# Two diffusion-mixer layers on one core: a re-ordered first norm, three first weight tiles instead of two, and prepared tables ahead of the first copies

## The reference

```python
ada_lat = silu_c @ ada_w[l] + ada_b[l]       # 1024 -> 6*1024: shift, scale, gate, twice
ada_ctx = silu_cc @ ada_w[l] + ada_b[l]
h  = rms_norm(x,  lp["ln1"]) * (1.0 + sc1)  + sh1     # latent tokens
hc = rms_norm(xc, lp["ln1"]) * (1.0 + csc1) + csh1    # context tokens
z  = h @ w_in                                # 1536 columns, in 12 tiles of 128
# columns of z: attention (low-rank q, kv, shared rotary key), Fourier, S5 state space
a_bar = exp(dt * a);  b_bar = ((a_bar - 1) / a) * b   # S5 tables: powers of a_bar times b
```

## Time and profile before

| | |
|---|---|
| median of 3 runs | 2171.99 us (2169.01 to 2174.01) |
| profiled execution | 2170.0 us, of which span of the trace 2168.1 us |
| PE | busy 2125.3 us, 98% of the span |
| DVE | 1228.1 us, 57% |
| POOL | 903.7 us, 42% |
| ACT | 505.2 us, 23% |
| mean granted TensorE clock | 0.995 |

### The profile page before, as it was taken

The page is one execution under the profiler, slowest core; times in us unless marked ns, Lnnn a source line. Parts: engine busy times, 40 slices in busy tenths (PEclk is TensorE's granted clock), DMA queues, the critical chain, the costliest instruction groups (busy, mean ns, idle before and its releaser), DMA issues.

```text
span 2168.1 us, 30631 instructions
## 1 busy us (share of the span) xinstructions
PE 2125.3 (98%) x12532; PEld 1897.7 (88%) x12532; DVE 1228.1 (57%) x1859; ACT 505.2 (23%) x814; POOL 903.7 (42%) x492
## 2 busy tenths in 40 slices
PE   6999999999999999999999999999999999999998
PEld 4999999877799899999999999888777787888886
DVE  7998981455663546454565424594266757263353
ACT  3115121454300220110201111322265212010010
POOL 2441443200243354444444443455411456766662
PEclk9999999999999999999999999999999999999999
DMA  7363354233553332122233254545310552322331
GB/s 282 100 141 101 116 191 145 88 120 120 199 192 138 133 122 88 59 78 88 78 88 103 92 204 187 120 153 195 127 39 23 197 182 88 107 97 97 97 97 68
DMA packets 105390, 267.80 MB, mean 124 GB/s; under 512 B 22650, under 2 KB 42490, under 8 KB 103470
## 3 DMA queue, kind: packets, MB, share of 16 engines
q1 hardware_dynamic: 68928, 190.87, 25.9%
q10 hardware_dynamic: 36334, 75.07, 10.5%
HBM read 227.56 MB, written 37.88 MB: 122 GB/s over the span
## 4 chain that ended last, share of the span: by engine, by line
PE 89%; DVE 8%; DMA 1%; ACT 1%; issue 1%; SPq 0%; POOL 0%; DVEq 0%; POOLq 0%; ACTq 0%
PE ps L482 67%; PE ps L1062 3%; PE ps L936 2%; PE ps L1076 2%; PE ps L1112 2%; PE ps L600 2%; PE ps L491 2%; DVE t_out L2233 2%; DVE t_in L2233 1%; PE ps L795 1%; PE ps L962 1%; PE ps L974 1%; PE ps L497 1%; PE ps L1009 1%; PE ps L925 1%; DMA ada_first<-in_ada_w 1%
## 5 line engine op out<-in xcount | busy, mean ns | idle before, releaser
L1304 POOL TENSOR_SCALAR whi<-raw 128x1024 fp32r<-128x1024 f32 x244 | 273.5, 1121 | 1212.1 <-PE ps L482 665.3
L1307 POOL TENSOR_TENSOR wlo<-raw,whi 128x1024 fp32r<-128x1024 f32 x244 | 630.7, 2585 | 20.3
L482 PE MATMUL ps<-hh,whi 128*128 128x384 f32 (+1 forms) x1560 | 462.8, 353 | 0.3 <-DVE ada L626 0.3
L482 PE MATMUL ps<-hl,whi 128*128 128x384 f32 (+1 forms) x1560 | 460.0, 351 | 0.0
L482 PE MATMUL ps<-hh,wlo 128*128 128x384 f32 (+1 forms) x1560 | 459.8, 351 | 0.0
L482 PEld LDWEIGHTS ps<-hh,whi 128*128 128x128 f32 x1560 | 283.6, 188 | 21.1 <-ACT mr L1737 1.0
L482 PEld LDWEIGHTS ps<-hl,whi 128*128 128x128 f32 x1560 | 285.3, 188 | 18.6 <-issue 0.2
L482 PEld LDWEIGHTS ps<-hh,wlo 128*128 128x128 f32 x1560 | 285.0, 188 | 18.4
L2166 DVE SCALAR_TENSOR_TENSOR x<-ps,ada,x 128x384 f32<-128x384 f32 (+1 forms) x160 | 80.5, 546 | 335.1 <-PE ps L482 335.0
L482 PE MATMUL ps<-midh,whi 128*128 128x384 f32 (+1 forms) x768 | 231.3, 355 | 1.8 <-DVE midl L2196 1.8
L482 PE MATMUL ps<-midl,whi 128*128 128x384 f32 (+1 forms) x768 | 229.7, 353 | 0.0
(11 more groups left out here) (259 smaller groups left out, 2954.9 us busy)
## 6 DMA issues: line engine op xcount, KB each, us to landing
raw<-in_w_main SPq DMA_DIRECT2D x244, 512.0 KB, 3.3
ada_gap<-in_ada_w SPq DMA_DIRECT2D x40, 512.0 KB, 10.1
ada_mixer<-in_ada_w SPq DMA_DIRECT2D x32, 512.0 KB, 4.0
g_d<-gt ACTq DMA_DIRECT2D x24, 384.0 KB, 2.4
gl<-g_d ACTq DMA_DIRECT2D x8, 1152.0 KB, 6.2
ada_first<-in_ada_w SPq DMA_DIRECT2D x16, 512.0 KB, 15.4
cout_d<-cz SPq DMA_DIRECT2D x12, 512.0 KB, 5.0
cout<-cout_d ACTq DMA_DIRECT2D x6, 1024.0 KB, 9.3
```

The costliest lines, as they stand in the source:

```text
L482: ins = pe.matmul(bank(p, h, a, b), ww[:, w % W_SLOTS, kw * P:(kw + 1) * P], xx[:, kx, a:b], start=(first and i == 0 and j == 0), stop=(la ...
L1304: pool.tensor_scalar(whi[:, u, :], raw[:, u % 2, :], 1.0, 0.0, ALU.mult, ALU.add).then_inc(w_split.sem, 1)
L1307: pool.tensor_tensor(wlo[:, u, :], raw[:, u % 2, :], whi[:, u, :].bitcast(F32), ALU.subtract).then_inc(w_split.sem, 1)
```

## The change

1. **DMA order.** The S5 input matrix (b_in, 384 KB) leaves the very start and is issued by ACT in the middle of the first norm. Weight tile 2 is loaded ahead of ada steps 12 to 15. Each ada step of the first 16 has a semaphore of its own, not one for two.
2. **Sums.** DVE adds all eight squares; PE sums once (6 matmuls in the program, not 12). PE then runs ada steps 4 to 6, spreads the first 512 tokens, runs step 7 and spreads the rest.
3. **Gain.** The part of the gain that doesn't depend on c, (ada_b + 1) * ln, is formed early (`first_gain_constant`, two small operations); later the sums are multiplied by ln where they lie in PSUM and added to it (`first_gain`, two small operations in place of one).
4. **First part in two pieces.** For k = 0 the first 512 tokens are handed from DVE to ACT and from ACT to PE on signals of their own.
5. **Power table.** Doublings 1 and 2 move from ahead of the first norm to behind its k = 3; doubling 4 moves to behind k = 7. POOL starts the split of tile 2 only after doubling 2.
6. **Three tiles.** PE takes tiles 0 and 1 through k = 0 to 3, with ada steps 8-10, 11-12 and 13-15 behind k = 0, 1, 2 and the turn of the second ada block behind the high part of k = 3; then tile 2 through k = 0 to 3, then tiles 0 to 2 together through k = 4 to 7. Tile 3 uses PSUM region 3, and the waits of tiles 3 to 6 follow.
7. **Copies later.** DVE does `inverses` and `input_weights` ahead of the three `inputs`, and all three of these ahead of `table_rows`.

```diff
-IN_PAIRS = ((0, 1, 2, 0, 1, 2, 0, 1, 2, 0, 1, 0), ...
+IN_PAIRS = ((0, 1, 2, 3, 1, 2, 0, 1, 2, 0, 1, 0), ...
+        def pe_first_sums(pe):
+            key = (0, 1)
+            pe.wait_ge(sq_used.sem, sq_used.at((key, KD - 1)))
+            for b in range(TOK // P):
+                ins = pe.matmul(ps[:, norm_pair(key), 2 * b:2 * b + 2], sqa[:, b * P:b * P + P], ones[:, 0:2], ...
+        def pe_first_spread(pe):
+            pe.wait_ge(diag_ready.sem, diag_ready.at(key))
+            pe.matmul(ps[:, norm_pair(key), 0:512], ones[:, :], diag[:, 0:512], start=True, stop=True)
+            pe_ada(pe, 7)
+            pe.matmul(ps[:, norm_pair(key), 512:TOK], ones[:, :], diag[:, 512:TOK], ...
+            pe_turn(pe, 0)
-            pe.wait_ge(ada_full[slot].sem, ada_full[slot].at(s | 1 if s < 8 * ADA_FIRST else s))
+            pe.wait_ge(ada_full[slot].sem, ada_full[slot].at(s))
+        def first_gain(dve, i):
+            dve.tensor_tensor(o, o, ln[...]..., ALU.mult)        # o lies in PSUM
+            dve.tensor_tensor(g, o, g, ALU.add)
...
 # pe_layer, l == 0
-                for k, steps in ((0, range(8, 11)), (1, range(11, 14))):
-                    first_tiles(range(2), k)
+                for i in range(2):
+                    wait_w(pe, i)
+                    for h, a, b in halves_of(TOK):
+                        pe.wait_ge(hi_ready.sem, hi_ready.at((0, 1, 0) if h else "piece"))
+                        for ww in (whi, wlo):
+                            pe.matmul(bank(i, h, a, b), ww[:, i, 0:P], hh[:, 0, a:b], start=(ww is whi), stop=False)
+                pe.wait_ge(lo_ready.sem, lo_ready.at((0, 1, 0)))
+                for i in range(2):
+                    low_step(pe, i, i, 0, TOK)
+                for k, steps in ((0, range(8, 11)), (1, range(11, 13)), (2, range(13, 16))):
+                    if k:
+                        first_tiles(range(2), k)
                     for s in steps:
                         pe_ada(pe, s)
...
-                for k in range(3, KD):
-                    first_tiles(range(2), k)
-                pe.wait_ge(ada_ready.sem, ada_ready.at(1))
-                tile(2, 2)
-                pe.wait_ge(in_dve.sem, in_dve.at((0, 0)))
-                tile(3, 0)
+                wait_w(pe, 2)
+                pe.wait_ge(ada_ready.sem, ada_ready.at(("gain", 0, 0, 4)))
+                for k in range(4):
+                    first_tiles((2,), k)
+                for k in range(4, KD):
+                    first_tiles(range(3), k)
+                tile(3, 3)
                 pe.wait_ge(in_dve.sem, in_dve.at((0, 1)))
                 tile(4, 1)
+                pe.wait_ge(in_act.sem, in_act.at((0, 3)))
                 halves(0)
...
 # POOL, split
+                if not t0 and u == 2:
+                    pool.wait_ge(prep_dve.sem, prep_dve.at((0, "power", 2)))
...
 # dve_layer, l == 0
                 dve_norm(dve, 0, 1, TOK, 0, KD // 2)
+                doubled(dve, 0, 1)
+                doubled(dve, 0, 2)
+                dve_ada(dve, 1)
+                first_gain(dve, 1)
+                dve_norm(dve, 0, 1, TOK, KD // 2, KD)
                 doubled(dve, 0, 4)
-                dve_ada(dve, 1)
-                dve_gain(dve, 0, 0, KD // 2, KD)
-                dve_norm(dve, 0, 1, TOK, KD // 2, KD)
-                inputs(0)
-                inputs(1)
                 inverses(dve, 0)
                 input_weights(dve, 0)
+                for i in range(3):
+                    inputs(i)
                 table_rows(dve, 0)
-                input_tables(dve, 0, 0)
-                inputs(2)
-                for c in range(1, S5_PARTS):
+                for c in range(S5_PARTS):
                     input_tables(dve, 0, c)
...
 # DVE, at the very start
             coefficients(dve, 0)
-            for k in range(1, KD - 1):
+            for i in range(2):
+                first_gain_constant(dve, i)
+            for k in range(1, 4):
                 add_squares(dve, (0, 1), k, TOK)
             transition(dve, 0)
-            doubled(dve, 0, 1)
+            for k in range(4, KD):
+                add_squares(dve, (0, 1), k, TOK)
             invert(dve, (0, 1), TOK)
-            doubled(dve, 0, 2)
```

More of the change, by code:

```diff
@@ L579, in ada_slot @@
             if s < 8 * ADA_FIRST:
[L580 removed]
+                return ada_first[s], s
             s -= 8 * ADA_FIRST
@@ L797, in chunk_inputs @@
                 ins.then_inc(bu_done.sem, bu_done.mark((l, q)))
-            for i in range(2):
-                wait_w(pe, t0 + i)
+            if l:
+                for i in range(2):
+                    wait_w(pe, t0 + i)
             if l == 0:
-                for k, steps in ((0, range(8, 11)), (1, range(11, 14))):
-                    first_tiles(range(2), k)
+                for i in range(2):
[10 more added lines that the diff above has]
+                        first_tiles(range(2), k)
@@ L1219, in _ @@
                 pe_ada(pe, s)
[L1220 to L1226, removed]
+            pe_first_sums(pe)
+            for s in range(4, 7):
+                pe_ada(pe, s)
+            pe_first_spread(pe)
             for l in range(DEPTH):
@@ L1254, in _ @@
             load_w(1)
-            for step in range(KD, 2 * KD):
+            for step in range(KD, KD + 4):
                 load_ada(step)
-            for t in range(2, n_all):
+            load_w(2)
+            for step in range(KD + 4, 2 * KD):
+                load_ada(step)
+            for t in range(3, n_all):
                 load_w(t)
@@ L1359, in act_hi @@
             at_ = ada_tile(0 if w == 1 else 3, k)
-            act.wait_ge(nt_ready.sem, nt_ready.at((l, w, k)))
+            pieces = (l, w, k) == (0, 1, 0)
+            act.wait_ge(nt_ready.sem, nt_ready.at("piece" if pieces else (l, w, k)))
             for s, (a, b) in enumerate(spans(n)):
+                if pieces and s:
+                    act.wait_ge(nt_ready.sem, nt_ready.at((l, w, k)))
                 ins = act.activation(hh[:, k, a:b], nt[:, k % 2, a:b], ACT.Identity, bias=ada[:, l, at_, s:s + 1])
+                if pieces and s == 0:
+                    ins.then_inc(hi_ready.sem, hi_ready.mark("piece"))
             ins.then_inc(hi_ready.sem, hi_ready.mark((l, w, k)))
@@ L1369, in act_layer @@
                     act_hi(act, 0, 1, TOK, k)
+                act.dma_start(s5[0].b_in[:], A["ssm_b"][0]).then_inc(prep_loaded.sem, prep_loaded.mark(0, 16))
                 act_rows(act, 1)
@@ L1835, in dve_norm @@
                                                    ps[:, norm_pair((l, w)), a:b], ALU.mult, ALU.mult)
+                    if (l, w, k, s) == (0, 1, 0, 0):
+                        ins.then_inc(nt_ready.sem, nt_ready.mark("piece"))
                 ins.then_inc(nt_ready.sem, nt_ready.mark((l, w, k)))
@@ L2387, in _ @@
             coefficients(dve, 0)
-            for k in range(1, KD - 1):
+            for i in range(2):
+                first_gain_constant(dve, i)
+            for k in range(1, 4):
                 add_squares(dve, (0, 1), k, TOK)
             transition(dve, 0)
-            doubled(dve, 0, 1)
+            for k in range(4, KD):
+                add_squares(dve, (0, 1), k, TOK)
             invert(dve, (0, 1), TOK)
-            doubled(dve, 0, 2)
             dve_ada(dve, 0)
-            dve_gain(dve, 0, 0, 0, KD // 2)
+            first_gain(dve, 0)
             for l in range(DEPTH):
```

40 lines of the change are left out of this document (28 added, 12 removed).

## The result

The changed kernel takes 2175.62 us (median of 20 runs, 2170.03 to 2179.29) against 2172.02 (20 runs, 2168.54 to 2174.97) for the kernel before in the same session: ratio 1.0015, 95% interval [1.0009, 1.0021]. It is slower by 0.15%, where 2168.0 was forecast, and above the upper end of the range, 2173.2. The profiled execution took 2174.04 us, of which the span 2171.9, 3.8 more than before.

A forecast was written before the change was run, and what follows sets the result against it. PE was taken as the bound, fed by DVE at `halves(0)`: start 2.65 us earlier, at 81.0, plus the final wait of 1.35 gone, made 4.0 off 2171.99, so 2168.0 us; range 2164.5 to 2173.2.

The forecast's parts named there:

- Views and bounds: PE and DVE run side by side to `halves(0)`; PE's 77.75 us from there to 161.40 is touched by no edit.
- Start, sums, two pieces: Up to the first norm: first nt at 29.8 instead of 31.65, PE starting at 31.35 on the smaller first piece.
- DVE to bin part 0: DVE from 55.5: 18.7 us of work without splits, 6.8 for splits, so bin part 0 ends at 81.0.
- The term for splits: DVE's table work before bin part 0: POOL's splits of tiles 4 to 8 cost it 6.8 us.
- the 1.6 us forecast: PE's stall ahead of the first transposes: it arrives at 79.4 and bin part 0 comes at 81.0.
- what I gave 9%: Rival, chance 0.09: PE stalls 6.4 us before `halves(0)`, its clock falls, 2.4 us slower, 2174.4 us.
- Its point of decision: PE's stall before `halves(0)`: the rival of the fallen clock decides from a stall near 3 us.
- The wait for cz: Ahead of PE's last `pe_kernels`: the final wait of 1.35 us for DVE's output tables goes.
- All three that I had named as signs of being wrong: DVE loses over 9 us to splits between 57 and 81, PE waits ahead of tile 4, granted clock falls after 60 us.
- 1.5 us of slack: PE at tile 4, waiting for the copy of tile 1: 69.6 against 71.1.
- the second rival: Splits fall in full on DVE: bin part 0 at 85.8, 0.9 us later at `pe_kernels` 5, 2172.9 us; chance 0.16.

The follow-up runs named there:

- e6: The changed kernel run again with nothing altered; 1.0014 of the kernel before.
- e10: e7 with POOL's split of tile 2 waiting for doubling 4 instead of doubling 2; 0.9984 of the kernel before.
- e4: The changed kernel with 20 more matmuls of 384 columns in PE's wait ahead of the first transposes; 1.0006 of the kernel before.
- e2: The changed kernel with each group of SP's stores of output tables and kernels one weight load earlier; 1.0006 of the kernel before.
- e13: The changed kernel with the earlier stores of e2 and the filled wait of e4; 1.0005 of the kernel before.
- e12: e10 with the earlier stores of e2; 0.9977 of the kernel before.
- e14: e10 with nine more matmuls in PE's wait ahead of the first tiles and the earlier stores of e2; 0.9976 of the kernel before.
- e7: The changed kernel with doublings 1 and 2 back around the inversion and doubling 4 in DVE's wait ahead of the second turn; 0.9992 of the kernel before.
- e1: The changed kernel with POOL's split of tile 4 waiting until DVE has made the input weights; 1.0011 of the kernel before.

## Why the prediction was wrong

**Views and bounds: right.** Two chains meet at `halves(0)`, and PE's way from there is constant while its clock stays up: 76.49 to 76.68 us to kernels 4 in those twelve profiles.

**Start, sums, two pieces: right, or better.** First nt at 29.33 (29.8 forecast), PE's first at 30.98 (31.35), the second turn at 43.5 (44.9, as I had counted the low clock, which this execution lacked), DVE waiting 3.13 (4.0), norm end 54.8 (55.5), tile 3 at 61.52 (62.8). That the turn came early was luck: in e6, the same kernel, it came at 46.04.

**The failed step: DVE to bin part 0.** The term for splits, 6.8 us, was 11.1. (The work beside it was sized right: its parts add up to 18.6, not 18.7.) In its parts: input weights 5.6 (I had 2.8 and 0.4), `table_rows` 2.6 (0.4), bin part 0 2.9 (2.5 and 0.7; tile 8's split did this, while tile 7's fell on `table_rows`). Two errors are in it. One: three of the four 64-partition copies do wait. The Trainium skill, SBUF — State Buffer, "Who interferes with whom", says that copies can enter a two-port mode and then take the lock too; I had quoted the rule for it and still priced them by their shape. The measurement agrees with the page for those three, 1.85 for 0.38; the fourth took 0.60 beside a split and without. Two: because POOL and DVE work back to back, being blocked makes DVE late enough to meet the next split as well: tile 5's was to fall on copies from PSUM, which are free, and fell on the last two of the weights. e10 shows the reverse. Instead of 81.0 bin part 0 came at 84.48, so the transposes start 0.98 later and not 2.65 earlier.

**The stall.** With it went the 1.6 us forecast, which became 4.67, and what I gave 9%: PE's clock fell behind the stall. That rival's mechanism was right, and its price near: 1.5 forecast, 1.26 measured (against e4 1.4; in e6 2.6). Its point of decision, 3 us, isn't tested at this place, where every wait was under 1.4 or over 4.6; ahead of the first tiles and of vsb the clock fell behind shorter ones. Its chance was wrong: I tied it to a stall of 6.4 us, each split in full, where one of 4.67 did.

**What no rival had.** From the first transposes on I took PE's way as untouched. It wasn't: SP's stores end later, ACT's vsb waits 2.72, PE 1.54, and the clock falls again, 1.71: together +3.25. In e2 and e13 both are gone. Of the 8.0 us between the forecast for the profiled execution, 2166.0, and its 2174.04, 3.6 are the late transposes, 1.0 PE's way from there to the state inputs (79.8 for 78.8), and 3.3 the state inputs. DVE's wait for the stores at 142.16 (4.03 us) shows the same queue. The wait for cz did go (-1.54), as forecast.

**The signs.** All three that I had named as signs of being wrong came: over 9 us lost to splits, a fallen clock behind 60 us, and PE waiting ahead of tile 4, 1.36 us at 71.36, where I had counted 1.5 us of slack. The last cost nothing, since PE stood for bin part 0 behind it. And the range ended at 2173.2, where the second rival that should bound it stood at 2172.9, and below the 2174.4 of a rival to which I gave 9%.

**Left open.** Why the clock from 31 to 38 us is 1.00 in some executions and near 0.5 in others behind the same idle time; why the stage's rest is 1995 to 1996 us in e2 and e12 and not in e14. A kernel whose table work has no SBUF operands beside a split wasn't tried.

## What to carry to other kernels

Where two engines exclude each other, count the collisions from a drawn-up timeline of both, with each delay fed back into the next meeting; an average of free and blocked cases is too kind, and moving 1.7 us of work was worth some 5 us here by the ratios (e7), and 7 with two splits held back (e10). Put work into a wait that the trace shows, not behind it. When PE gets a lead over an engine that feeds it, price the stall, the clock behind it and every queue in the following stage that was in time by less than the shift.

## What the runs showed of the hardware

- Behind 2.30 to 2.48 us of idle PE ahead of the first tiles, the granted clock was below 0.8 from 31 to 35 or from 35 to 38 us in nine of twelve profiles of changed kernels without a fill, and 1.00 in all three with nine matmuls in the gap (0.55 to 1.16 us idle). In one of the nine, e7, it was 1.00 from 31 to 35 and 0.74 from 35 to 38, behind a second wait of 2.19 us. Ahead of the first transposes and the last `pe_kernels` it fell behind each wait of 4.67 to 4.93 us and behind none of 0.36 to 1.39. At the wait for vsb length alone doesn't tell: it fell behind 1.54 in the changed kernel and stayed at 1.00 behind 2.51 in e6.
- A fallen clock may stay down while the trace has PE busy throughout: 8.00 us at 0.50 in e1.
- Three of DVE's four fp32 copies from SBUF to SBUF on 64 partitions wait for POOL's split: 0.94, 1.09, 1.85 for 0.35, 0.36, 0.38. The fourth (432 elements, read in reversed order, as is the second) took 0.60 in the first layer of all sixteen profiles, also beside wlo; the memset (0.46) didn't wait either.
